# Middle's order in a decoder-layer kernel: sample's projections in other banks, a query projection ahead of the first convolution chunks, and four pieces of sample's work a step later

## The reference

```
proj = x @ w_in + b_in                       # q | k | v | conv value | conv gate
attn = window_attention(rope(q), rope(k), v) # window 128, 8 heads, 2 kv heads, sinks
u    = ca * sigmoid(cg)
conv = silu(layer_norm(depthwise_conv31(u)))
mix  = concat(attn, conv) @ w_out + b_out
h    = layer_norm(alpha * x + mix)
y    = layer_norm(alpha * h + hier_moe(h))   # top-1 group of 4, top-2 of its 8 experts
```

## Time and profile before

| | |
|---|---|
| median of 3 runs | 1373.07 us (1369.31 to 1374.18) |
| profiled execution, its own time | 1375.28 us |
| its span in the trace | 1373.4 us |
| TensorE busy | 1257.1 us, 92% |
| VectorE busy | 740.0 us, 54% |
| ScalarE busy | 537.3 us, 39% |
| POOL busy | 471.0 us, 34% |
| mean granted TensorE clock | 0.966 of 2.4 GHz |

### The profile page before, as it was taken

One profiled execution on the slowest core, in us unless ns is written; L12 is line 12 of the kernel. 1 busy time (PEld: TensorE's weight loads), 2 busy tenths in 40 slices (PEclk: granted clock), 3 DMA queues, 4 the chain that ended last, 5 costly groups with the idle time before them and its releaser, 6 DMA issues.

```text
span 1373.4 us, 21264 instructions
## 1 busy us (share of the span) xinstructions
PE 1257.1 (92%) x5579; PEld 603.3 (44%) x5580; DVE 740.0 (54%) x2093; ACT 537.3 (39%) x883; POOL 471.0 (34%) x633
## 2 busy tenths in 40 slices
PE   8999997889999998799999999999999999999910
PEld 3444444657666655445555545433333333333300
DVE  2423433463655564748888888544444444444338
ACT  0000001333444443423333332265566666566544
POOL 5113110000000000245555554365565566656321
PEclk9999998999999998999999999999999999999965
DMA  6365554222112166246666554279999999999776
GB/s 254 93 221 158 180 152 157 73 97 69 63 62 77 55 196 186 92 141 216 213 215 219 158 154 124 86 226 318 311 291 368 338 286 332 328 367 362 197 265 262
DMA packets 91256, 273.41 MB, mean 199 GB/s; under 512 B 14888, under 2 KB 41088, under 8 KB 78038
## 3 DMA queue, kind: packets, MB, share of 16 engines
q1 hardware_dynamic: 73975, 226.53, 46.6%
q0 software_dynamic: 14384, 42.32, 12.8%
q10 hardware_dynamic: 2807, 3.53, 0.8%
HBM read 212.80 MB, written 66.40 MB: 203 GB/s over the span
## 4 chain that ended last, share of the span: by engine, by line
PE 46%; issue 30%; DVE 11%; DVEq 5%; DMA 4%; ACT 1%; POOL 1%; POOLq 1%; SPq 1%; ACTq 0%
PE P L1117 13%; PE bank_S L1139 9%; PE M L1117 6%; PE bank_S L737 4%; PE P L737 3%; DVEq L1705 2%; PE bank_T L737 2%; PE M L737 2%; DMA work<-conv_rows 1%; DVE route L1710 1%; PE M L1125 1%; DVE work L1667 1%; PE bank_S L911 1%; DMA big<-sum_rows 1%; ACT work L1429 1%
## 5 line engine op out<-in xcount | busy, mean ns | idle before, releaser
L1379 ACT ACTIVATE big<-big 128x2048 f32 x76 | 145.1, 1910 | 121.8 <-issue 74.6
L1117 PE MATMUL P<-big,work 128*64 x416 | 188.0, 595 | 1.8 <-DVE work L1923 1.5
L1118 PE MATMUL P<-big,work 128*64 128x512 f32 x416 | 188.0, 595 | 0.0
L776 PE MATMUL P<-big,work 128*128 128x256 f32 (+1 forms) x512 | 173.6, 496 | 0.0
L2114 POOL DMA_INDIRECT work<-h_rows,piece_idx x148 | 142.1, 960 | 62.9 <-issue 40.1
L1139 PE MATMUL bank_S<-big,work 128*64 x304 | 136.7, 592 | 1.0 <-DVE work L1907 1.0
L1141 PE MATMUL bank_S<-big,work 128*64 128x512 f32 x304 | 136.7, 592 | 0.0
L2030 POOL TENSOR_SCALAR work<-work 128x1 f32<-128x1 f32 (+1 forms) x17 | 3.8, 222 | 380.0 <-DVE work L1588 380.0
L776 PEld LDWEIGHTS P<-big,work 128*128 128x128 f32 x512 | 97.3, 194 | 70.4 <-issue 63.6
L911 PE MATMUL P<-big,work 128*128 128x512 f32 x256 | 116.4, 608 | 5.0 <-DVE work L1624 5.0
L911 PE MATMUL bank_S<-big,work 128*128 128x512 f32 x256 | 113.8, 597 | 0.0
(11 more groups left out here) (356 smaller groups left out, 2269.4 us busy)
## 6 DMA issues: line engine op xcount, KB each, us to landing
big<-in_w SPq DMA_DIRECT2D x96, 1024.0 KB
work<-in_xt_prompt SPq DMA_DIRECT2D x32, 512.0 KB, 4.3
big<-sum_rows SPq DMA_DIRECT2D x16, 520.0 KB, 8.4
big<-in_toe SPq DMA_DIRECT2D x16, 512.0 KB, 3.3
work<-in_x_prompt SPq DMA_DIRECT2D x16, 512.0 KB, 3.9
h_rows<-work SPq DMA_DIRECT2D x16, 512.0 KB, 2.7
sum_rows<-work SPq DMA_DIRECT2D x16, 512.0 KB, 3.6
out_y_prompt<-big SPq DMA_DIRECT2D x16, 512.0 KB
```

What stands on the lines that cost most here:

```text
L776: last = mm(dst[0:n, 0:c1 - c0], lhs[:, k, :], w_qkv[:, k, c0:c1], start=(k == 0), stop=(k == KD - 1))
L1117: mm(lower, xgT[j][:, k, 0:U], both[:, k], start=(k == 0), stop=(k == KD - 1))
L1118: last = mm(upper, xgT[j][:, k, U:P], w_up[:, k], start=(k == 0), stop=(k == KD - 1))
L1379: fn(w_up.rearrange("p k m f -> p m k f")[:, :, ks, :], src, ACT.Copy).then_inc(s[f"wu{part}_ok"], 1)
```

## The change

Seven edits, all in the order or in the place of results:

1. `project_sample` writes all four quarters to M0 instead of P0 and P1. TensorE therefore no longer waits for `c_ev` (the last readout of the stretch before) ahead of the Middle; the wait stands before the first query projection.
2. Chunks 0 and 1 of the convolution go from step 0 into step 1, behind that query projection. Chunks 2 and 3 stand together behind the key/value projection of step 1.
3. Pieces 4, 5 and 6 of sample are done in steps 5, 6, 7 instead of 4, 5, 6 (`SAMPLE_AT`), and piece 9 in step 10; statistics, normalisation, gain, swish and mix of sample also move one step on.
4. `project_out_sample` writes its four quarters to columns 0 to 255 of P1 alone.
5. `project_out(1, 0)`, into P0, no longer waits for `o0_ev`.
6. `turn_z(1)` goes ahead of the transposes of step 17 (first half).
7. On ScalarE `normal_conv(2)` goes ahead of the copy of the last attention output.

```diff
@@ -389,6 +389,7 @@
         OUT = [PAIR[0]] + [PAIR[c % 2 == 0] for c in range(1, NT + 1)]
+        SAMPLE_AT = {1: 1, 2: 2, 3: 3, 5: 4, 6: 5, 7: 6, 10: 9}
         BY_PE = (0, NT - 1, NT)
         h_parts = flat_ptB
...
@@ -780,7 +781,7 @@
                 lhs = xT_of(load)
                 for k in range(KD):
                     for q in range(4):
-                        last = mm((P0, P1)[q // 2][quarter_rows(q), 0:QKV // 4], lhs[:, k, :],
+                        last = mm(M0[quarter_rows(q), 0:QKV // 4], lhs[:, k, :],
                                   w_qkv[:, k, q * QKV // 4:(q + 1) * QKV // 4], start=(k == 0), stop=(k == KD - 1))
                 last.then_inc(s["pe_x"], 1)
...
@@ -880,7 +881,7 @@
 
-            SAMPLE_DONE = {9: ("zl_ok", 1), 2: ("sA_ev", 2), 3: ("sB_ev", 1), 4: ("sB_ev", 2), 5: ("sB_ev", 3), 6: ("sB_ev", 4)}
+            SAMPLE_DONE = {10: ("zl_ok", 1), 2: ("sA_ev", 2), 3: ("sB_ev", 1), 5: ("sB_ev", 2), 6: ("sB_ev", 3), 7: ("sB_ev", 4)}
 
...
@@ -894,15 +895,15 @@
                 after(pe, s["mix_ok"], c)
                 for k in range(KD):
                     for q in range(4):
-                        at = 256 * (q % 2)
-                        last = mm(OUT[c][q // 2][quarter_rows(q), at:at + 256], mix_sT[:, k, :], w_out[:, k, 256 * q:256 * (q + 1)],
+                        last = mm(P1[quarter_rows(q), 0:256], mix_sT[:, k, :], w_out[:, k, 256 * q:256 * (q + 1)],
                                   start=(k == 0), stop=(k == KD - 1))
                 last.then_inc(s["pe_o1"], 1)
 
             def project_out(c, half, sem):
                 n = rows_of(OUT_IN[c])
                 lhs = mix_of(c)
-                after(pe, s[f"o{half}_ev"], 0 if c == 1 else c - 2)
+                if (c, half) != (1, 0):
+                    after(pe, s[f"o{half}_ev"], 0 if c == 1 else c - 2)
                 for k in range(KD):
                     if k == 0 and half == 0:
                         pe.wait_ge(s[f"am_in{c % 2}"], 16 * ((c - 1) // 2 + 1))
...
@@ -979,7 +980,6 @@
 
             pe.wait_ge(s["const_in"], 16)
             pe.wait_ge(s["wqkv_in"], 16)
-            after(pe, s["c_ev"], NT)
             for step in range(STEPS):
                 t = step - 2
                 I, S, VB = step <= NT, 0 <= t < NT, 0 <= t - 1 < NT
@@ -1003,23 +1003,30 @@
                     project_sample(load)
                 elif I:
                     pe.wait_ge(*x_landed(load))
-                    after(pe, s["q_ev"], step - 1)
+                    if step == 1:
+                        after(pe, s["c_ev"], NT)
+                    else:
+                        after(pe, s["q_ev"], step - 1)
                     project_in(P0, load, 0, AD, s["pe_q"])
-                if 1 <= step <= 9:
+                if step == 1:
+                    for chunk in CHUNK_OF[0]:
+                        conv_part(chunk, 0)
+                        conv_part(chunk, 1)
+                if step in SAMPLE_AT:
                     if VB:
                         after(pe, s["at_ev"], t - 1)
-                    sample_piece(step)
-                if step == 1:
-                    conv_part(chunks[0], 0)
-                    conv_part(chunks[0], 1)
+                    sample_piece(SAMPLE_AT[step])
                 if I and step:
-                    after(pe, s["kv_ev"], step - 1)
+                    if step > 1:
+                        after(pe, s["kv_ev"], step - 1)
                     project_in(P1, load, AD, QKV, s["pe_x"])
                 if step == NT + 1:
                     after(pe, s["q_ev"], NT)
                     after(pe, s["kv_ev"], NT)
                     pe.wait_ge(s["w_out_in"], 16)
                     project_out_sample(0)
+                    after(pe, s["cv_ev"], CHUNKS - 1)
+                    turn_z(1)
                 if S:
                     if step in SAMPLE_DONE:
                         name, count = SAMPLE_DONE[step]
@@ -1027,17 +1034,12 @@
                     after(pe, s["pA_ok"], t)
                     after(pe, s["scB_ev"], t)
                     flip(bank_T, smA, s["pe_fA"])
-                if step == 0:
-                    conv_part(chunks[0], 0)
+                if step == 1:
+                    for chunk in chunks:
+                        conv_part(chunk, 0)
+                        conv_part(chunk, 1)
+                elif step and chunks:
                     conv_part(chunks[0], 1)
-                if step <= 1:
-                    conv_part(chunks[1], 0)
-                    conv_part(chunks[1], 1)
-                elif chunks:
-                    conv_part(chunks[0], 1)
-                if step == NT + 1:
-                    after(pe, s["cv_ev"], CHUNKS - 1)
-                    turn_z(1)
                 if S:
                     after(pe, s["ptA_ev"], t)
                     after(pe, s["at_ev"], t - 1)
@@ -1283,6 +1285,8 @@
                         act.wait_ge(s["g_init"], 1)
                     fn(qT.rearrange("p g t -> p (g t)"), bank_S[:, 0:AD], ACT.Copy)
                     fn(kT2[:, (t % 2) * P:(t % 2 + 1) * P], bank_S[:, AD:AD + P], ACT.Copy).then_inc(s["T_ev"], 1)
+                if step == NT + 2:
+                    normal_conv(2)
                 if VB:
                     after(act, s["pe_vB"], t - 1)
                     after(act, s["at_st"], t - 2, per=16)
@@ -1290,11 +1294,11 @@
                 if S:
                     exps(smA, 0, s["nmA_ok"], s["expA_ok"], t)
                     exps(smB, G, s["nmB_ok"], s["expB_ok"], t)
-                if 1 <= step <= 6:
-                    sample_piece(step)
-                if step == 8:
+                if step in SAMPLE_AT and step < 10:
+                    sample_piece(SAMPLE_AT[step])
+                if step == 9:
                     normal_conv(0)
-                if step == 10:
+                if step == 11:
                     swish_conv(0)
                 if S:
                     after(act, s["pe_fA"], t)
...
@@ -1314,7 +1318,7 @@
             for c in range(NT + 3):
                 if 0 <= c - 1 < NT:
                     scale_h(c - 1)
-                if c + 2 <= NT:
+                if 3 <= c + 2 <= NT:
                     normal_conv(c + 2)
                 if 2 <= c + 1 <= NT:
                     swish_conv(c + 1)
...
@@ -1619,9 +1623,9 @@
                     last = stt(r[b][0:n, cols], xb[b][0:n, cols], ALPHA, OUT[c][half][0:n, :], ALU.mult, ALU.add)
                 else:
                     for q in (2 * half, 2 * half + 1):
-                        rows, at = quarter_rows(q), 256 * (q % 2)
+                        rows = quarter_rows(q)
                         cols = slice(256 * q, 256 * (q + 1))
-                        last = stt(r[b][0:n, cols], xb[b][rows, cols], ALPHA, OUT[c][half][rows, at:at + 256], ALU.mult, ALU.add)
+                        last = stt(r[b][0:n, cols], xb[b][rows, cols], ALPHA, P1[rows, 0:256], ALU.mult, ALU.add)
                 last.then_inc(s[f"o{half}_ev"], 1)
 
             def norm_h(c):
...
@@ -1743,11 +1747,11 @@
                     sample_max()
                 if step == 4:
                     sample_norm()
-                if step == 7:
+                if step == 8:
                     conv_stats(0)
-                if step == 9:
+                if step == 10:
                     gain_conv(0, M0)
-                if step == 11:
+                if step == 12:
                     mix_conv(0)
                 if step == NT:
                     conv_stats(1)
```

More of the change, by code:

```diff
@@ L1730, in _ @@
                             rows, lo, hi = quarter_rows(q), q * part, min((q + 1) * part, AD + KVD)
-                            last = tt(qk[0:n, lo:hi], (P0, P1)[q // 2][rows, 0:hi - lo], b_qkv[rows, lo:hi], ALU.add)
+                            last = tt(qk[0:n, lo:hi], M0[rows, 0:hi - lo], b_qkv[rows, lo:hi], ALU.add)
                         last.then_inc(s["q_ev"], 1)
@@ L1759, in _ @@
                         rows = quarter_rows(3)
-                        tt(v_s[0:n, :], P1[rows, part - KVD:part], b_qkv[rows, AD + KVD:], ALU.add).then_inc(s["kv_ev"], 1)
+                        tt(v_s[0:n, :], M0[rows, part - KVD:part], b_qkv[rows, AD + KVD:], ALU.add).then_inc(s["kv_ev"], 1)
                     else:
```

## The result

The changed kernel takes 1360.98 us (median of 4 runs, 1358.64 to 1362.54); the kernel before, on the same chip, takes 1373.62 us (4 runs). The ratio is 0.991, 95% interval 0.9886 to 0.9935: about 0.9% faster. The profiled execution took 1360.41 us with a span of 1358.6 us and a mean clock of 0.973; before it was 1375.28, 1373.4 and 0.966. The profiled pair differs by 14.9 us (forecast 15.5), the medians by 12.6 us. The predicted 1358.7 us is 2.3 us under the measured median, within the forecast's range of 1354 to 1363.

The account below looks back on a forecast made before the run. TensorE bounds the Middle; in output projection and router TensorE and VectorE are both near their limit. 1.2 + 6.7 + 7.6 = 15.5 us off 1375.28 gives 1359.8, less half of 2.2: 1358.7 us, range 1354 to 1363.

Parts of the forecast that it names:

- B: Step 4: piece 4 of sample, a step later, no longer waits for VectorE and the clock stays up; 6.7 us faster.
- C: End of the Middle: project_out(1, 0) runs without its wait at full clock and VectorE's loads come earlier; 7.6 us faster.
- A: Steps 0 and 1: the reordered projections and chunks let chunk 4 start at 248.0 instead of 249.20; 1.2 us faster.
- its tile landed 6.4 us later: Step in A: the query projection's tile, issued at 213.62, lands 6.4 us later, so dense work begins at 220.0.
- The 2.0 us for the clock: Cost in A: after TensorE's idle time before 220.0, 4 us at half clock cost 2.0 us.
- The 3.2 us for the clock: Part of B: without the wait in step 4 the clock stays full, saving 3.2 us besides the 3.74 us wait.
- The margins: In C, before the output projection needs them: attention columns land 1.7 us early, mix_conv(1) is done 0.3 us early.
- The unseen cost: Sample's four quarters writing one bank instead of two: taken as 0, at the upper end twice as long.
- Rival 1: At A, B and C only the waits go, the clock falls elsewhere: 8.5 us faster, 1365.7 us; chance 0.14.
- Rival 2: The router stage absorbs C, leaving it 0 to 2 us: 8.9 us faster in all, 1365.3 us; chance 0.09.
- Rival 3: Steps 0 to 2: the clock stays down through dense projections; 8 us slower than before, 1382.3 us; chance 0.03.
- Half of the 2.2 us: Whole kernel: the profiled execution before was 2.2 us over the runs' median; half of that was taken off the forecast.

Follow-up runs that it names:

- e1: The kernel before with only the edits of steps 0 and 1 (sample projection in M0, query projection ahead of chunks 0 and 1); 1370.67 us, ratio 0.9979.
- e9: e4 plus three products with unused results in TensorE's wait for chunk 4's Toeplitz load; 1357.84 us, ratio 0.9889 to the kernel before.
- e3: The kernel before with only the edits at the end of the Middle; 1365.24 us, ratio 0.9945.
- e2: The kernel before with only sample's pieces 4, 5, 6 and 9, and what hangs on them, one step later; 1366.80 us, ratio 0.9943.
- e4: The changed kernel without its edits in steps 0 and 1; 1360.65 us, ratio 0.9911 to the kernel before.
- e8: The changed kernel with turn_z(1) and normal_conv(2) back at their old places; 1357.94 us, ratio 0.9892 to the kernel before.
- e11: The changed kernel run again, unaltered, on the same chip as e12; 1358.35 us, ratio 0.9902 to the kernel before.
- e6: The changed kernel plus seven products with unused results between sample projection and first query projection; 1355.61 us, ratio 0.9872 to the kernel before.
- e5: The changed kernel with the last three 512 KB writes of zeros moved to step 1; 1353.58 us, ratio 0.9857 to the kernel before.
- e7: The changed kernel with the zero writes of e5 and four filling products like those of e6; 1355.37 us, ratio 0.9878 to the kernel before.
- e12: e7 run again beside e11 on the same chip; 1353.16 us, ratio 0.9856 to the kernel before.

## Why the prediction was right, step by step

The number came out right; of its three parts B and C were right in their mechanism, and A was right by luck.

- **A.** Forecast 1.2 us (bounds -1.2 to 3.2); about 1.3 over the profiled executions, -0.3 in the recorded pair, and by the medians 0.0 to 0.4% (e1), not told from nothing on top of B and C. The size fits, its make-up doesn't, so that it fits is luck. The step "its tile landed 6.4 us later" failed: it was issued 2.2 us behind the end of stretch 1 (2.0 before), but took 7.8 us, which put the query projection 10.1 us behind the end of stretch 1, where I had 8.4. The 2.0 us for the clock came out as 9.42 - 7.13 = 2.3. The sample projection, freed from its wait, ran in 2.78 us, which only made the wait longer. What seems to make up for this is a term that I did not have: the fall of the clock behind the 2.60 us wait, absent in the one execution that I read, present in the other four without A. Step 2 is 2.4 to 3.3 us longer with it (23.9 to 24.8 against 21.5), and in e9's profiled execution filling the wait was worth as much as the whole of A. I had even taken the clock of 1.00 at 245 to 250 as evidence against rivals 1 and 3.
- **B.** Forecast 6.7 us; 6.45 in the profiled pair, 5.5 against step 4 of e1 and e3, and e2 alone gives 0.57%, with an interval that holds all of these. The 3.2 us for the clock were read from one execution; in two others they are 2.1. The pieces, one step later, cost 0.4 us over steps 5 to 10, where I had 0.2. No new wait appeared.
- **C.** Forecast 7.6 us; 8.1 in the recorded pair, 7.2 between e1, e2 and e3, e4, 5.4 to 7.7 by the wait and the projection alone, and e3 alone gives 0.55%. The margins held: the attention columns landed about 1 us before they were needed (I had 1.7), and there is no wait for mixing. The load of the convolution rows followed the attention copy as said; VectorE's wait for it ended 14.9 us earlier, where I had "some 15 us earlier".
- **The unseen cost.** Four quarters in one bank: 64 matmuls take 3.64 us (558.95), to the hundredth what they took in two banks before:

```profile
565.95 3.64 PE L898 MATMUL P<-big,smp 128*8 128x256 f32 x64
```

My upper end, twice as long, isn't there; the value taken, 0, is right. The 4.47 us that I measured it against held half clock (granted clock 0.62 over 213.6 to 218.1).

- **Rival 1** falls with the clock at 1.00 at 306 and 579 and with e2 and e3. **Rival 2** falls with e3: the router stage gave back none of C (776.2 us from VectorE's statistics to the end of the span, 776.6 before). A small part of its mechanism is real: TensorE's lead beyond VectorE's is swallowed (e8), as I wrote. **Rival 3**: the clock was at half for 6.8 us from 220.2 and back at 227, as before (10.2 us in e1 and e11, but back before the query projection ended); the three gaps of 0.79 us did not keep it down. Its price in the text is 0.1 us off: 1375.28 + 8.0 - 1.1 is 1382.2.
- **Half of the 2.2 us.** The profiled execution before was 1.7 us over the median of its 4 runs here, the one after 0.6 under; these two distances are the 2.3 us between the pair's 14.9 and the medians' 12.6. The half that I took off was near what was needed, but it stood on no measurement; the 1.4 us of step 15, which no edit touches, are of the same kind.

The Trainium skill, "TensorE: Matmul & The Clock Gate", Part 1, says that the array is at 1.2 GHz by default and is released by activity. The query projection of e6, after seven products that nobody needs, took 7.13 us where it took 9.42 without them: the trace agrees, with 2.3 us for the projection. By that rule alone, though, I called this edit a bad trade, and no run shows it to be one: it exchanged up to three stretches at half clock in steps 0 to 2 (213.8 in some executions, 220.7, and 248 in four of five) for one (220.2).

## What to carry to other kernels

A wait's price is the wait and what the clock does behind it, and the second part varies between executions. Before a wait is written off as short, look at the clock behind it in more than one execution; one profile can lack the fall that most others have. Where a wait can't be removed, dense products whose results nobody uses can keep the clock up through it: one to four lines, and in the profiled executions worth as much as the new order of steps 0 and 1. When a consumer is put first, look at the issue and the landing of its data and at what else is in the queues just then, because these set its start. Where two engines are near their limits, a lead of the one that waits may be worth nothing, as here (e8).

## What I had not expected of the hardware

- The same wait of 2.6 us at 248 was followed by no fall of the clock once, and by half clock for 6.8 to 10.2 us in four other profiled executions.
- The length of one kernel's runs goes with its mean granted clock. Of 46 runs of the kernel before, the 9 with a clock of 0.964 or less took 1374.0 to 1379.8 us, the 7 with 0.970 or more 1366.1 to 1373.5.
- Clock matters to eight-row products with 192 columns: 64 of them took 2.78 or 2.79 us where the clock stayed, 4.2 to 4.5 us where it fell; the 64-column convolution products took 2.51 to 2.58 either way.
- The same load of 512 KB landed after 6.4 us in the kernel before, 7.4 to 8.2 in the five kernels with A and the zeros early, and 7.0, 5.0 and 5.7 with the zeros later (e5, e7, e12). Moving two writes from ahead of it and one from behind it did not bring it to the 3.8 us (changed; 4.3 before) that is the median of all such loads.
